# A hybrid convolution and sparse-attention layer: stage ends regrouped, splits and copies moved between VectorE, ScalarE and GpSimd, attention blocks 0 to 4 rearranged

## The reference, cut to what matters

```python
proj = x @ w_in                  # q | k | v | indexer q, k, weights | conv gates B, C | conv input h
scores = sum_h w_h * relu(qi_h @ ki.T)          # top 256 keys of each row, causal
attn = softmax(q @ k.T / 8 over the chosen keys) @ v          # 8 heads x 64, rotary on q and k
conv = B * causal_conv3(C * h)
mix  = concat(rms_norm(attn), rms_norm(conv)) * g
x    = layer_norm(alpha * x + mix @ w_out)
x    = layer_norm(alpha * x + (silu(x @ w_gate) * (x @ w_up)) @ w_down)
```

## Time and profile before

| | |
|---|---|
| median of 3 runs | 1369.96 us (1367.16 to 1370.05) |
| profiled execution | 1363.54 us, span 1361.8 us |
| mean granted clock of TensorE | 0.992 of full |
| PE busy | 1310.7 us, 96% of the span |
| DVE, ACT, POOL busy | 657.8, 417.6, 538.1 us |
| index scores | about 61 to 134 us |
| rest of the projection | 134 to 381 us |
| attention | 381 to 529 us |
| mixing product | 530 to 628 us |
| feed-forward | 628 to 1349 us |
| last norm and stores | to the end |

### The profile page before, as it was taken

How to read it: one execution, slowest core, us unless ns; L and a number is a source line. 1 busy time by engine, 2 the same in 40 slices (tenths; PEclk the granted TensorE clock), 3 DMA queues, 4 the chain that set the end, 5 groups by cost and what they waited for, 6 DMA issues and landing times.

```text
span 1361.8 us, 16816 instructions
## 1 busy us (share of the span) xinstructions
PE 1310.7 (96%) x6385; PEld 1102.2 (81%) x6385; DVE 657.8 (48%) x1217; ACT 417.6 (31%) x731; POOL 538.1 (40%) x398
## 2 busy tenths in 40 slices
PE   8979999999988999999999999999999999999996
PEld 8957888888878887877888888888888888888885
DVE  3677999999958886267021203030303030212126
ACT  3466222222477886123302021111111111111115
POOL 2320667996776321046423141322323232232226
PEclk9989999999999999999999999999999999999998
DMA  5330112211011024122010111102020201010103
GB/s 187 78 86 16 47 47 55 78 47 32 16 39 40 17 78 140 47 93 93 31 62 32 62 35 58 66 27 92 0 92 7 86 31 62 31 62 31 31 0 124
DMA packets 67537, 76.82 MB, mean 56 GB/s; under 512 B 3460, under 2 KB 54936, under 8 KB 67480
## 3 DMA queue, kind: packets, MB, share of 16 engines
q1 hardware_dynamic: 67480, 76.08, 18.5%
HBM read 64.53 MB, written 4.19 MB: 50 GB/s over the span
## 4 chain that ended last, share of the span: by engine, by line
PE 86%; DVE 6%; POOL 3%; ACT 1%; issue 1%; DMA 1%; SPq 0%; POOLq 0%; DVEq 0%; ACTq 0%
PE banks L496 25%; PE banks L498 25%; PE banks L497 25%; PE banks L710 2%; PE banks L761 2%; DVE scores L1591 1%; POOL y L1499 1%; PE banks L661 1%; PE banks L732 1%; PE banks L731 1%; PE banks L678 1%; DMA gu_raw<-in_w_gate_up 1%; POOL v_hl L1387 1%; PE banks L679 1%; DVE y L1823 1%
## 5 line engine op out<-in xcount | busy, mean ns | idle before, releaser
L496 PE MATMUL banks<-act_hi,gu_hi 128*128 128x512 f32 x704 | 274.1, 389 | 0.0
L498 PE MATMUL banks<-act_hi,gu_lo 128*128 128x512 f32 x704 | 273.9, 389 | 0.0
L497 PE MATMUL banks<-act_lo,gu_hi 128*128 128x512 f32 x704 | 273.9, 389 | 0.0
L1858 DVE TENSOR_TENSOR h_f<-banks,silu 128x512 f32<-128x512 f32 x40 | 27.7, 692 | 408.5 <-ACT silu L1151 408.5
L1445 POOL TENSOR_TENSOR h_lo<-h_f,h_hi 128x1024 fp32r<-128x1024 f32 x21 | 50.5, 2406 | 343.6 <-ACT h_hi L1155 331.9
L1607 DVE TENSOR_SCALAR_CACHE_REDUCE mask<-scores,small 128x384 bf16<-128x384 f32 (+1 forms) x186 | 163.7, 943 | 1.1
L1863 DVE TENSOR_TENSOR y<-banks,y 128x1024 f32<-128x1024 f32 x80 | 98.0, 1225 | 118.7 <-PE banks L498 118.7
L1440 POOL TENSOR_TENSOR gu_lo<-gu_raw,gu_hi 128x1024 fp32r<-128x1024 f32 x44 | 105.5, 2420 | 124.1 <-ACT gu_hi L1143 124.1
L498 PEld LDWEIGHTS banks<-act_hi,gu_lo 128*128 128x128 f32 x704 | 132.2, 188 | 27.4
L496 PEld LDWEIGHTS banks<-act_hi,gu_hi 128*128 128x128 f32 x704 | 132.2, 188 | 27.3
L497 PEld LDWEIGHTS banks<-act_lo,gu_hi 128*128 128x128 f32 x704 | 132.2, 188 | 27.3
(11 more groups left out here) (226 smaller groups left out, 2415.2 us busy)
## 6 DMA issues: line engine op xcount, KB each, us to landing
gu_raw<-in_w_gate_up SPq DMA_DIRECT2D x22, 1024.0 KB, 7.0
wd_raw<-in_w_down SPq DMA_DIRECT2D x11, 1024.0 KB, 5.0
w_raw<-in_w_in SPq DMA_DIRECT2D x32, 192.0 KB, 2.7
w_raw<-in_w_in SPq DMA_DIRECT2D x24, 256.0 KB, 2.9
xs<-in_x SPq DMA_DIRECT2D x8, 512.0 KB, 5.2
wo_raw<-in_w_out SPq DMA_DIRECT2D x16, 256.0 KB, 5.7
x_res<-in_x SPq DMA_DIRECT2D x16, 256.0 KB, 2.7
out<-y SPq DMA_DIRECT2D x8, 512.0 KB, 2.6
```

The lines of the kernel that those rows point to most:

```text
L496: pe.matmul(dst, a[0], b[0], start=first, stop=False)
L497: pe.matmul(dst, a[0], b[1], start=False, stop=False)
L498: return pe.matmul(dst, a[1], b[0], start=False, stop=last)
L1858: dve.tensor_tensor(h_f[:, j, cols_], ps[:, 2 * half + 1, :], silu[:, cols_], ALU.mult).then_inc(h_done, 1)
```

## The change

Eight edits, by stage:

- **Index scores.** SP spreads the queries of blocks 2 and 3 together ahead of weight load 22, where block 3 stood behind loads 22 to 27.
- **Attention, start.** `v_high(1)` and `split_v(1)` move into the projection's end; `v_high(0)` goes ahead of the last two `copy_out`; block 0's values get their low part from DVE (`split_first_v`, at i = 1) and not from POOL, which takes `root_conv`, `split_v(1)` and then the queries of block 1 as soon as the projection has ended. `copy_q` of blocks 2 to 5 goes from ACT to DVE.
- **Convolution split.** `conv_high` and `conv_lower` work in halves of 512 columns, in the order 2, 3, 0, 1 of the parts: ACT at i = 16, 17, 19, 20, 22, 23, 27, 28 behind the exponentials, DVE (parts 0 and 1) at i = 24, 25, 29, 30 where it was i = 18 and 20. Parts 2 and 3 stay with POOL at i = 27.
- **Block 3's sum** in two halves of four heads, at i = 32 and, behind the turned parts, at i = 35. PE's first value product of block 4 waits for the first half only.
- **Attention, end.** The first four `wo_high` and `wo_lower` move into the unit loop. PE starts `mix(0)` before the last `fold_parts`; the last block's sum and norm stand behind the `wo_lower` on DVE; the last turn is behind `mix(2)`.
- **End of the mixing product.** PE's turns follow three blocks behind, not two; `turn_x1(5)` stands between the first two parts of `first_gate_up`, and DVE's `x1_lower(4)` behind the last `norm`.
- **Last norm.** DVE finishes blocks 6 and 7 with one instruction each (block 7 in two halves), with the bias from PSUM, where ACT copies it (`BIAS2`). ACT and POOL finish 0 to 5 only, and block 5's bias is behind the last root.
- **Stores** follow: blocks 0 to 4, 6, 7 in halves, then 5.

```diff
             for s in range(KT, NSLOT):
                 if s == 22:
-                    spread_idx(SEL[0])
+                    for b in SEL[:2]:
+                        spread_idx(b)
                 elif s == 28:
-                    for b in SEL[1:]:
+                    for b in SEL[2:]:
                         spread_idx(b)
...
             for b in range(NB):
                 mix(NB + b)
-                if b >= 2:
-                    turn_x1(b - 2)
+                if b >= 3:
+                    turn_x1(b - 3)
...
                 gate_up_part(0, 0, 0, 0, 0)
+                turn_x1(NB - 3)
                 gate_up_part(0, 0, 1, 0, 0).then_inc(gu_ready, 1)
...
             mix(0)
+            fold_parts(NU - 1)
             mix(1)
+            mix(2)
             turn(("o", NB - 1))
-            for m in range(2, NB):
+            for m in range(3, NB):
                 mix(m)
...
             for n in range(4):
                 split_q(0, n)
-            split_v(0)
+            root_conv()
+            split_v(1)
             for n in range(4):
                 split_q(1, n)
-            for b in range(1, 4):
+            for b in (2, 3):
                 split_v(b)
...
+            def split_first_v():
+                dve.wait_ge(v_hi, 2)
+                dve.tensor_tensor(v_hl[:, 0, :, 1, :], v_raw[:, 0, :].rearrange("p (h d) -> p h d", h=HEADS),
+                                  v_hl[:, 0, :, 0, :].bitcast(F32), ALU.subtract).then_inc(v_lo_first, 1)
+
+            def copy_q(b):
+                dve.wait_ge(qt_ready, b + 1)
+                dve.tensor_copy(q_raw[:, b, :], Q_BANK[b]).then_inc(qt_copied2, 1)
...
-                if i == LARGE0 + 3:
-                    sum_heads(SMALL - 1)
+                if i == LARGE0:
+                    sum_last_small(0)
                 for c in chunks[i]:
                     turned_low(c)
-                if i in (18, 20):
-                    conv_lower((18, 20).index(i))
+                if i == LARGE0 + 3:
+                    sum_last_small(1)
+                if 2 <= TURN_AT.get(i - 1, 0) < 6:
+                    copy_q(TURN_AT[i - 1])
+                if i - 2 in CONV_AT[4:]:
+                    conv_lower(CONV_AT.index(i - 2))
...
             for b in range(NB):
-                if b >= 3:
-                    x1_lower(b - 3)
+                if b >= 4:
+                    x1_lower(b - 4)
                 add_residual(NB + b)
...
             norm(NB - 1)
+            x1_lower(NB - 4)
             x1_lower(NB - 3)
...
-            dve.tensor_tensor(y[:, NB - 1, :], y[:, NB - 1, :], bias2[:], ALU.add).then_inc(biased, 1)
+            for b, first, n in ((NB - 2, 0, DM), (NB - 1, 0, DM // 2), (NB - 1, DM // 2, DM // 2)):
+                dve.wait_ge(gained2, b + 1)
+                dve.wait_ge(root_ready, NB + b + 1)
+                dve.scalar_tensor_tensor(y[:, b, first:first + n], scaled[:, b % 2, first:first + n],
+                                         rstd[:, b % 2:b % 2 + 1], BIAS2[:, first:first + n], ALU.mult, ALU.add
+                                         ).then_inc(finished, 1)
```

195 lines of the change are left out of this document (119 added, 76 removed).

## The result

| | before | with the change |
|---|---|---|
| median | 1368.38 us (19 runs, 1364.1 to 1372.2) | 1354.53 us (19 runs, 1353.3 to 1366.4) |
| profiled execution | 1363.54 us, span 1361.8 | 1354.53 us, span 1352.7 |
| mean granted clock there | 0.992 | 0.994 |

The ratio is 0.991, with an interval of 0.9897 to 0.9923: faster by about 0.9%. The profiled executions differ by 9.1 us, where the sum said 9.3. The medians differ by 13.9 us. This difference of about 5 us between two ways to compare is a result of its own, and the experiments take it up.

The account below looks back on a forecast made before the run. PE was taken as the bound, busy 1310.7 of 1361.8 us. Terms 3.3 + 2.5 + 3 - 0.5 + 2 + 2.5 - 6 + 2.5 gave 9.3 us: 1369.96 to 1360.7 us median, range 1353.5 to 1367.5.

Parts of the forecast that it names:

- block 3: Attention block 3: loss 0.5 us (bounds 0 and 2) from VectorE's four half subtractions, set against its 5.6 us idle.
- block 4: Attention block 4: gain 2 us (bounds 1 and 2.5) from PE's shorter wait for VectorE's sum of block 3.
- attention's end: Attention's end: gain 2.5 us (bounds 1 and 3), the first low weights coming before the last values.
- end of the mixing product: Mixing product's end: loss 6 us (bounds 3 and 9), PE standing at turn_x1(5): 6.4 + 1.5 - 2.
- block 2: Attention block 2: gain 3 us (bounds 1 and 4), VectorE's convolution subtractions leaving it and ScalarE's copies split.
- rival 1: Mixing product's end: no stand at turn_x1(5), loss near nothing; gain 15.3 us, 1354.7 us; chance 12%.
- Index scores: Index scores: gain 3.3 us (bounds 2.3 and 4.5), block 3's low queries spread ahead of the weight loads.
- tail: Kernel's tail: gain 2.5 us (bounds 1.5 and 3.5), the last root no longer behind GpSimd's bias.
- Blocks 0 and 1: Attention's start: gain 2.5 us (bounds 1 and 3), GpSimd splitting block 1's queries earlier, query copies moving to VectorE.
- I take the gain to be the same there: Whole kernel: the profiled execution's gain of 9.3 us also holds for the median, 6.4 us longer.
- The second: Attention: VectorE's new work eats ScalarE's savings; blocks 0 to 4 gain 1.5 us, not 7; 1366.2 us; chance 18%.
- The third: Blocks 0 to 3: VectorE becomes the bound, five instructions each losing 2.06 us to GpSimd; 1374.6 us; chance 6%.

Follow-up runs that it names:

- experiment 11: Changed kernel with VectorE's x1_lower(4) and x1_lower(5) ahead of the last norm and all four convolution low parts on GpSimd: 1341.55 us.
- experiment 1: Kernel before with only the end-of-mixing edit (turns three blocks behind, x1_lower(4) behind the last norm): median 1371.7 us, ratio 1.0024 against before.
- experiment 6: Changed kernel with the copies of the turned queries of blocks 2 to 5 on ScalarE again: median 1364.9 us.
- experiment 5: Changed kernel with the convolution's split at its old places, in copies and subtractions of 1024 columns: median 1353.9 us.
- experiment 8: Changed kernel with the low part of block 0's values made by GpSimd again, not VectorE: median 1361.4 us.
- experiment 4: Changed kernel with all four convolution low parts on GpSimd and VectorE's half subtractions left out: median 1350.6 us, ratio 0.9873 against before.
- experiment 2: Changed kernel with the end-of-mixing edit alone taken back: median 1355.7 us.
- experiment 3: Changed kernel with PE's new order kept, but VectorE's x1_lower(4) and x1_lower(5) put ahead of the last norm: median 1350.5 us.

## Why the prediction was right, and where its steps were off

**The sum.** 9.3 us were forecast for a profiled execution and 9.1 came, but this nearness is in part luck. By the table above, four rows came out 4.7 us worse than their terms (block 3 by 2.2, the first dots by 1.3, block 4 and the attention's end by 0.8 and 0.4), the others 4.5 us better (the end of the mixing product by 1.7, block 2 by 1.6). For the median, 9.3 us were forecast and 13.9 came (the step is below); that it is in the range is luck as well, since the range reached so low for rival 1.

**Index scores, attention's end, tail.** 3.3, 2.5 and 2.5 us were forecast; 4.0, 2.1 and 2.5 came, each by the mechanism named. Of the 1 us set against the index scores for VectorE beside GpSimd 0.3 came: its first two sums took 0.69 and 0.81 us, 0.48 and 0.75 before. The first dots began 1.3 us later in the profile after, which the sum did not have. That is no price of the change: over all profiles they begin between 64.6 and 66.2 us, at 64.63 in experiment 11, which starts as the changed kernel does, and at 66.19 in experiment 1, which starts as the one before.

**Blocks 0 and 1.** 2.5 forecast, 2.9 came. About 0.8 us are the copies (experiment 6), and 0.4 us of block 1 go with the convolution's split (experiment 5). The rest is the place of the queries on GpSimd: experiment 8 shows that this sets block 0, but the rest's own size is only what is left over. The step "units 0 to 7 shorten by about 1 us" held nearly, with 0.75. One sign failed: "No DMA wait before block 1's logits", where 0.83 us are left.

**Blocks 2 and 3.** Here a step failed. Block 2 gave 4.6 and not 3, outside its bounds; block 3 lost 2.7 and not 0.5, outside them too. The price of the halves was right in sum (0.81, 1.38, 0.68 and 0.68 us, together 3.55; 2.4 to 4.1 forecast), though the second was dearer than the 1.0 given to the dearest. Wrong was its cover: "VectorE had 5.6 us idle in the 35 us that hold blocks 3 and 4". That idle time lies in other units. At the start of block 3 VectorE also has block 1's norm, which took 1.48 us beside GpSimd, so that it was busy for 18.50 of 19 us, and PE waited for it three times, by 0.5 to 1.4 us. Experiment 4 shows the price of the halves there to be 3.0 us, against 3.55 us of their own length: little of it was covered. Together blocks 2 to 4 gave 3.1 us where 4.5 were forecast, and experiment 5 shows that the new places of the convolution's split brought nothing to the time on the whole.

**Block 4.** 2 forecast, 1.2 came.

**End of the mixing product.** The loss was forecast at 6 and was 4.3, inside 3 to 9, and the stand of 5 to 7 us was there with 6.92. The working divides it rightly but for one term. PE's slow matmuls took 2.6 us, not 1.5. And VectorE began its low parts 104.75 us behind `mix(0)` instead of 109.36, so 4.6 us sooner, where I took 2: the chain of the mix loop had waited for PE more than I gave it. 6.4 + 2.6 - 4.6 = 4.4, against 4.3 measured. What the forecast did not see is that the stand was not the price of PE's new order but of one place on VectorE: with the low parts ahead of the norm, PE's new order gains 5.0 us over the old one (109.82 in experiment 2, 104.83 in experiment 3).

**The median.** "I take the gain to be the same there" is the step that cost most: 4.6 us of gain. Another 1.6 us lie in the starting point, 1369.96, where 19 runs gave 1368.38. I had three runs, and the profiled execution was 6.4 us under their median; I took that for scatter. It was the granted clock: 0.992 in that execution, 0.982 to 0.987 in 21 of the 29 runs of the table. Of the changed kernel's 19 runs only 3 are at such a clock, so the medians gained more than the sum of the waits. Between the runs at the higher clock, 1363.1 to 1364.6 us before and 1353.3 to 1355.2 after, the gain is 9 to 10 us. The profile of before could have told that such falls are at hand, since the first two windows of the attention stood at 0.92 and 0.91.

**The rivals.** The first named the measured time, 1354.7 us, but not what happened: the stand was there. The second (attention does not pay) did not hold: blocks 0 to 4 gained 6.0 us, near the 7 forecast, though blocks 2 to 4 alone gave less than forecast. The third, VectorE as the bound in blocks 0 to 3, is what happened in block 3 alone. Its price of 2.06 us for each of five instructions did not come: the four halves lost 0.13, 0.70, 0 and 0 us against their length alone (0.68), and block 0's value split nothing (0.69). The Trainium skill, "SBUF — State Buffer", section "Who interferes with whom", lets one of the two engines wait for the whole instruction of the other. The rows agree with it, if the wait is for what is left of the other's instruction. GpSimd's bias ran to 619.49 and the gain pass, begun at 617.32, ended 1.1 us behind it, at 620.58; GpSimd's split, begun at 619.46, ended 2.20 us behind that, at 622.78; the bias pass ended 1.1 us behind the split, at 623.86. So the two engines took turns. The half that took 1.38 us fits too: it ended 0.55 us behind a split of the queries on GpSimd, which ran to 413.12. A half that meets only the end of an instruction loses little, so the price of a long pass was too much for it.

## What to carry to other kernels

Idle time of an engine covers new work only at the unit in which it lies: look at windows as short as the unit that gets the work, not at a sum over two blocks. When an order is changed on one engine, walk the engines that release it for the instruction that is behind the wrong neighbour; here three lines on VectorE turned a loss of 4 us into a gain of 5. And look at the granted clock of every run beside its time: a median of three over runs at two clocks can hide a gain of 4 us or show one that isn't there.

## What the runs showed of the hardware

- **Behind gaps of TensorE its clock can be at half for the next 25 us.** In experiment 6, ahead of the fall, PE was busy for 6.07 of 8 us; then it ran at 1.2 GHz, fully busy, until 443 us, and blocks 3 and 4 took 47.9 us in place of 36.9. The changed kernel's own profile has the same gaps (6.09 of 8 us busy) and no fall. With the gaps closed (15.52 of 16 us busy) no run had a mean clock under 0.99, in 14 runs of three kernels.
- **GpSimd is slowed as well as VectorE: they take turns.** Beside VectorE's passes GpSimd's bias took 2.85 us and not 2.39, its weight split 3.32 and not 2.41, while VectorE's two passes of two SBUF inputs took 3.26 and 3.25 and not 1.23. VectorE's two ended 1.1 us behind the end of GpSimd's instruction, GpSimd's two 2.20 us behind the end of VectorE's.
- **An instruction with one large input in SBUF is slowed too.** The first pass of the norm (`y` and a column of scalars) took 0.81 us alone, 1.13, 1.42, 1.72 and 1.93 us beside GpSimd's split in experiment 3, and ended 0.54 to 0.55 us behind the end of that split each time. The low part, with one input in PSUM, was not slowed (1.28 and 1.29 for two).
